# Between the two layers of a hybrid diffusion block: a new closing expert, gate rows in the routings, stores by SyncE, eight homes for the weight stream

## The reference, cut to what matters

```python
for l in range(DEPTH):
    ...
    h = modulate(rms_norm(x, g_pre_a), sh_a, sc_a)
    hc = modulate(rms_norm(xc, g_pre_a), csh_a, csc_a)
    mix, mix_c = token_mixers(h, hc, w_in[l], ...)
    x = x + gt_a * rms_norm(mix @ w_out[l], g_post_a)
    ...
    h = modulate(rms_norm(x, g_pre_f), sh_f, sc_f)
    x = x + gt_f * rms_norm(expert_choice_ffn(h, w_router[l], w_gate[l], w_up[l], w_down[l]), g_post_f)
    if update_ctx:
        ... the same for xc
```

## Time and profile before

| what | value |
|---|---|
| median of 3 runs (lowest, highest) | 2159.86 us (2159.2, 2161.35) |
| the profiled execution, its own time | 2164.66 us |
| its span, first to last instruction | 2162.9 us |
| PE busy / DVE busy / ACT busy / POOL busy | 89% / 25% / 22% / 8% |
| DMA over the span | 250 GB/s, 541.77 MB |
| mean granted TensorE clock | 0.952 of 2.4 GHz |

### The profile page before, as it was taken

The page is one execution under the profiler, slowest core; times in us unless marked ns, Lnnn a source line. Parts: engine busy times, 40 slices in busy tenths (PEclk is TensorE's granted clock), DMA queues, the critical chain, the costliest instruction groups (busy, mean ns, idle before and its releaser), DMA issues.

```text
span 2162.9 us, 25147 instructions
## 1 busy us (share of the span) xinstructions
PE 1916.5 (89%) x10460; PEld 892.7 (41%) x10460; DVE 545.7 (25%) x1168; ACT 473.5 (22%) x967; POOL 162.7 (8%) x230
## 2 busy tenths in 40 slices
PE   5998989999869999999997399879985989888885
PEld 2655545764423333333332255447632333332331
DVE  1021454761330000000000402456625011111113
ACT  4131113442311101111011513124421111111111
POOL 0000010100001011110101000011101000000000
PEclk9999989999979999999999699989997999999997
DMA  9221157002579999999999212110027999999994
GB/s 395 98 76 41 39 198 288 27 6 78 203 295 405 414 399 395 385 388 398 397 383 356 106 39 78 39 64 21 11 93 295 429 428 428 428 428 428 428 428 185
DMA packets 52750, 541.77 MB, mean 250 GB/s; under 512 B 6352, under 2 KB 8656, under 8 KB 23232
## 3 DMA queue, kind: packets, MB, share of 16 engines
q1 hardware_dynamic: 34400, 486.72, 54.9%
q0 software_dynamic: 18128, 53.95, 7.6%
q10 hardware_dynamic: 144, 0.01, 0.0%
HBM read 516.54 MB, written 24.12 MB: 250 GB/s over the span
## 4 chain that ended last, share of the span: by engine, by line
PE 72%; DMA 17%; DVE 6%; ACT 3%; issue 1%; POOL 0%; SPq 0%; DVEq 0%; POOLq 0%; ACTq 0%
DMA ring<-in_wstream 16%; PE ps L1694 15%; PE ps L1369 9%; PE ps L1757 7%; PE ps L1588 6%; PE ps L1702 5%; PE ps L1347 5%; PE ps L1536 3%; PE ps L1764 3%; PE ps L1474 2%; PE ps L1293 1%; PE ps L1339 1%; PE ps L1509 1%; PE ps L1502 1%; PE ps L1317 1%
## 5 line engine op out<-in xcount | busy, mean ns | idle before, releaser
L1694 PE MATMUL ps<-ring,work 128*64 128x512 f32 x2048 | 462.5, 604 | 38.4 <-DMA ring<-in_wstream 33.9
L1694 PEld LDWEIGHTS ps<-ring,work 128*64 128x64 f32 x2048 | 145.1, 139 | 349.9 <-issue 289.2
L1757 PE MATMUL ps<-big,work 128*64 128x512 f32 x1024 | 237.1, 605 | 3.1 <-ACT work L731 3.1
L1218 DVE TENSOR_TENSOR work<-glao,ps 128x512 f32<-128x512 f32 x32 | 22.0, 688 | 830.9 <-ACT glao L737 439.5
L1369 PE MATMUL ps<-hT,ring 128*128 128x512 f32 (+1 forms) x592 | 206.3, 507 | 1.9 <-DVE hT L880 1.4
L1369 PEld LDWEIGHTS ps<-hT,ring 128*128 128x128 f32 x592 | 112.0, 190 | 94.9 <-issue 86.4
L1588 PE MATMUL ps<-ring,hT 128*128 128x512 f32 x320 | 138.7, 592 | 0.0
L1757 PEld LDWEIGHTS ps<-big,work 128*64 128x64 f32 x1024 | 68.4, 138 | 140.2 <-issue 131.1
L1702 PE MATMUL ps<-ring,work 128*32 128x512 f32 x1024 | 119.8, 597 | 0.0
L1347 PE MATMUL ps<-ring,hT 128*128 128x384 f32 (+3 forms) x384 | 110.9, 450 | 0.0
L651 ACT ACTIVATE work<-ps,work 128x512 f32<-128x512 f32 (+2 forms) x120 | 82.0, 684 | 79.8 <-DVE work L1022 45.5
(11 more groups left out here) (256 smaller groups left out, 2020.4 us busy)
## 6 DMA issues: line engine op xcount, KB each, us to landing
ring<-in_wstream SPq DMA_DIRECT2D x166, 2048.0 KB, 12.7
big<-in_wstream SPq DMA_DIRECT2D x64, 2048.0 KB, 15.6
x_kept<-big POOLq DMA_DIRECT2D x14, 512.0 KB, 3.0
big<-x_kept POOLq DMA_DIRECT2D x14, 512.0 KB, 6.4
xn_lat<-big POOLq DMA_DIRECT2D x8, 512.0 KB, 10.8
big<-in_x_all SPq DMA_DIRECT2D x6, 512.0 KB, 6.4
work<-in_nat_bias POOLq DMA_DIRECT2D x16, 192.0 KB, 2.7
big<-in_x_all POOLq DMA_DIRECT2D x6, 512.0 KB, 6.9
```

The source lines that it names most:

```text
L1694: last = T.matmul(bank(m)[64 * h:64 * h + 64, :], XST[:, kc, e, 0:CAP_L], gate_up[j][:, kk, m * D + h * 512:m * D + (h + 1) * 512], start= ...
L1757: last = T.matmul(bank(3)[64 * g:64 * g + 64, :], HT[:, kc, 0:CAP_L], down[j][:, kc % 4, h * 512:(h + 1) * 512], start=kc == 0, stop=kc == ...
```

## The change

It has five parts.

1. **Gate rows of the expert stage** move into the routings: DVE builds the diagonals in layer 0 in `post_att`, in layer 1 at the end of `route`; PE multiplies and ACT copies them to `GROW_F` before the experts begin. PE waits for `grow_out` before its first gather transposes.
2. **Modulation units** are reordered: 12 under the attention, six (before: four) in layer 0's routing, of which the last two come after the indices are turned, none (before: two) between the layers.
3. **Layer 0's last expert** is written apart (`closing`): its context products come first, its context outputs are added on chip (`combine_ctx`), the context tiles are normed while PE computes the last latent down products; the latent outputs are added on chip too, together with the accumulators, by an identity product (`last_middle`). POOL scatters 15 experts, not 16, and reads the accumulators back before the last expert has ended. The next norm's scaling is folded into the transposing product (`turn_next`, with a scaled identity), two tiles at a time.
4. **Layer 1's experts** have eight homes for units (before six): the seventh in `big`, the eighth in two halves in `hT` and `work`. SP issues units 6 and 7 as soon as the first gathered rows are there. The programs of PE, ACT and SP for these experts are written out instead of looped. POOL reloads x for the closing norm when PE has used up unit 92 of 96 (before: all 96).
5. **Closing norm**: whole tiles of 1024 in one DVE addition, ACT's square-root table loaded beforehand, the result stored by SP.

```diff
-MOD_ROUTE = [[10, 11, 12, 13], [22, 23]]
-MOD_BOUND = [14, 15]
-MOD_ORDER = list(range(MOD_EARLY)) + MOD_ATT + MOD_ROUTE[0] + MOD_BOUND + MOD_ROUTE[1]
-MOD_GROUPS = [(0, 4), (4, 10), (16, 22), (10, 12), (12, 14), (14, 16), (22, 24)]
+MOD_ATT = list(range(4, 16))
+MOD_ROUTE = [list(range(16, 22)), [22, 23]]
...
+def laps(l, u):
+    if l < DEPTH - 1:
+        return u % SLOTS, u // SLOTS
+    return u % MORE, u // MORE + (NE if u % MORE < SLOTS else 0)
+def unit_used(l, n, j):
+    s, g = laps(l, SLOTS * n + j)
+    return ffn_used[s], g + 1
...
+for u in range(SLOTS, FFN_UNITS):
+    s, g = laps(l, u)
+    if g:
+        sp.wait_ge(ffn_used[s], g)
+    if s < MORE - 1:
+        sp.dma_start(ffn_slot(l, s), wstream[FFN_AT[l] + u, :, :]).then_inc(ffn_full[s], 16)
+    else:
+        for h in range(2):
+            sp.dma_start(home(l, s)[h], wstream[FFN_AT[l] + u, :, h * HALF:(h + 1) * HALF]).then_inc(ffn_full[s], 16)
...
+n = IN_AT[1] + i
+if i == 2:
+    for t in range(NLT):
...
             load(n)
+for t in range(NLT):
+    sp.wait_ge(sem("x_ready"), t + 1 + (DEPTH - 1) * NLT)
+    sp.dma_start(out[t * P:(t + 1) * P, :], X[:, t, :]).then_inc(sem("stored"), 16)
+sp.wait_ge(sem("stored"), 16 * NLT)
...
-for j in range(RING, SLOTS):
-    pool.wait_ge(ffn_used[j], (l + 1) * NE)
-for t in tiles(l):
+pool.wait_ge(*((ffn_used[4], NE) if ctx_too else unit_used(l, NE - 1, 2)))
...
+        scatter_add(2 * i + 1)
+for c in range(NCT):
+    pool.dma_start(X_CTX[:, c, :], xkeep[LAT + c * P:LAT + (c + 1) * P, :]).then_inc(sem(f"x_rows{NLT + c}"), 16)
+for c in range(NCT):
+    pool.wait_ge(sem(f"x_rows{NLT + c}"), 32)
+pool.wait_ge(sem("gather"), 3 * PAIRS)
+pool.wait_ge(sem("added"), ZERO_DMAS + 32 * (NE - 1))
 for t in tiles(l):
...
+        pool.dma_start(XN[:, t, :], src).then_inc(sem(f"x_rows{t}"), 16)
+    for t in range(NLT):
+        pool.wait_ge(sem(f"x_rows{t}"), ACC_READ)
+    x_again()
 else:
...
     modrow(n, SGL, bank(0))
+for j, n in enumerate(mods[4:]):
+    modrow(n, (SGL, SGC)[j], bank((0, 2)[j]))
+if not ctx_too:
+    act.wait_ge(sem("grow"), 1 + before("grow", l, "f"))
+    S.activation(GROW_F[0], ps[:, 2 * 512:4 * 512], ACT.Copy).then_inc(sem("grow_out"), 1)
 def picked(i, g):
     act.wait_ge(sem("gather"), i * (3 if ctx_too else 2) + (g + 1 + l * PER["gather"]))
...
+def closing(i, e):
+    act.wait_ge(sem("up_ctx"), 1)
+    S.activation(SGC[64:P, :], bank(2)[0:64, :], ACT.Silu).then_inc(sem("silu_ctx"), 1)
+    hidden_turned_ctx(i, e)
+    act.wait_ge(ffn_used[3], NE)
+    S.activation(SGL, bank(0), ACT.Silu).then_inc(sem("silu"), 1)
+    outputs_ctx(i, e).then_inc(sem("yev_ctx"), 1)
+    hidden_turned(i, e)
+    S.activation(AFM[:, 15:16], ones[:, 0:1], ACT.Sqrt)
+    output_square(l, NLT)
+    output_square(l, NLT + 1)
+    act.wait_ge(sem("cols"), 4 * (l + 1) + 2)
+    next_square(l, NLT)
+    outputs(i, e)
+    next_square(l, NLT + 1)
 def expert(i, e, last_pair):
...
+def post_middle(l):
+    output_square(l, 0)
+    output_square(l, 1)
+    act.wait_ge(sem("xT"), 1 + before("xT", l + 1, "a"))
+    h_next(range(KC // 2), 0)
+    next_square(l, 0)
+    h_next(range(KC // 2, KC), 0).then_inc(sem("h_ctx"), 1)
+    output_square(l, 2)
+    next_square(l, 1)
+    output_square(l, 3)
+    next_square(l, 2)
+    act.wait_ge(sem("xT"), 2 + before("xT", l + 1, "a"))
+    h_next(range(KC // 2, KC), 1).then_inc(sem("h_ctx"), 1)
+    next_square(l, 3)
+    act.wait_ge(sem("xT"), 4 + before("xT", l + 1, "a"))
+    h_next(range(KC // 2, KC), 2).then_inc(sem("h_ctx"), 1)
...
-    dve.wait_ge(sem("grow_out"), 1 + before("grow_out", l, half))
-    nxt = (l, "f") if half == "a" else (l + 1, "a")
-    if half == "f" and l == DEPTH - 1:
-        last_add(l, 0)
+def post_att(l):
...
+def new_x(i):
+    t = tiles(l)[i]
+    dve.wait_ge(sem("psq"), i + 1 + before("psq", l, "f"))
+    link(V.reciprocal(rs[:, t:t + 1], ss[:, t:t + 1]))
+    if t < NLT:
+        V.scalar_tensor_tensor(XN[:, t, :], ps[:, (t % 2) * D:(t % 2) * D + D], rs[:, t:t + 1], GROW_F[0], ALU.mult, ALU.mult)\
+            .then_inc(sem("y_used"), 1)
+        dve.wait_ge(sem("y_used"), t + 1 + before("y_used", l, "f"))
+        dve.wait_ge(sem(f"x_rows{t}"), X_AGAIN[l])
+        V.tensor_tensor(X[:, t, :], X[:, t, :], XN[:, t, :], ALU.add).then_inc(sem("x_ready"), 1)
     else:
-        dve.wait_ge(sem(f"x_rows{t}"), X_AGAIN[l])
-        done, n = ("x_ready", t + 1 + l * NLT) if t < NLT else ("xc_ready", t - NLT + 1)
-    V.tensor_tensor(X[:, t, :], X[:, t, :], GAIN_X, ALU.add).then_inc(sem(done), 1)
-    dve.wait_ge(sem(done), n)
-    if i and nxt[0] < DEPTH:
...
+new_x(0)
+new_x(1)
+normal(0)
+normal(1)
+for i in range(NCT, NT):
+    new_x(i)
+    if i > NCT:
+        normal(i - 1)
+dve.wait_ge(sem("xT"), 2 + before("xT", l + 1, "a"))
+h_next(range(KC // 2), 1)
+normal(NT - 1)
+dve.wait_ge(sem("xT"), 3 + before("xT", l + 1, "a"))
+h_next(range(KC // 2), 2)
...
+        mod_out(3, bank(1))
+    else:
+        dve.wait_ge(sem("mod_out"), 5)
+        gate_rows(l, "f")
 def ffn(l):
     ctx_too = l < DEPTH - 1
...
 last.then_inc(sem("logits"), 1)
 mods = MOD_ROUTE[l]
...
+for j, n in enumerate(mods[4:]):
+    mod_rows(n, bank((0, 2)[j]))
+for j, n in enumerate(mods[4:]):
+    mod_cols(n, (SGL, SGC)[j], bank(1))
+if l == DEPTH - 1:
+    gate_rows(l, "f")
...
-if ctx_too:
+    if ctx_too:
+        pe.wait_ge(ffn_full[j], i * 32 + 16 * (e + 1))
+    else:
+        s, g = laps(l, SLOTS * (2 * i + e) + j)
+        pe.wait_ge(ffn_full[s], (32 if s == MORE - 1 else 16) * (g + 1))
+if closing:
+    unit_in(0)
+    up_ctx(0)
+    up_lat(0).then_inc(ffn_used[0], 1)
+    unit_in(1)
+    up_lat(1)
+    up_ctx(1).then_inc(ffn_used[1], 1)
+    unit_in(2)
...
-        down_lat(1).then_inc(ffn_used[5], 1)
-pe.wait_ge(sem("mod_out"), (5, 7)[l])
+        down_lat(1).then_inc(used(5), 1)
+pe.wait_ge(sem("mod_out"), (4, 5)[l])
 pe.wait_ge(sem("xs_rows"), fetched(l, 1))
+pe.wait_ge(sem("grow_out"), 1 + before("grow_out", l, "f"))
 gather(0, 0)
 gather(0, 1)
...
+def last_middle(l):
+    def whole(t):
+        pe.wait_ge(sem(f"x_rows{t}"), ACC_READ)
+        if t == 0:
+            pe.wait_ge(sem("acc"), NCT)
+        elif t >= 2:
+            pe.wait_ge(sem("y_used"), t - 1 + before("y_used", l, "f"))
+        for h in range(2):
+            T.matmul(bank(2 * (t % 2) + h), ident, XN[:, t, h * 512:(h + 1) * 512], start=True, stop=False)
+        if t == 0:
+            pe.wait_ge(sem("yev"), NE)
+        for h in range(2):
+            r = slice(64 * h, 64 * h + 64)
+            last = T.matmul(bank(2 * (t % 2) + h), PT_L[0][r, t * P:(t + 1) * P], YL[1][r, :], start=False, stop=True)
+        last.then_inc(sem("comb"), 1)
+    def turn_next(i, b0):
+        t = tiles(l)[i]
+        pe.wait_ge(sem("xn"), i + 1 + before("xn", l + 1, "a"))
+        src = X[:, t, :] if t < NLT else X_CTX[:, t - NLT, :]
+        return [T.matmul(bank(b0, P, k * 2 * P + i % 2 * P), src[:, k * P:(k + 1) * P], NORM[t], start=True, stop=True) for k in range(KC)]
+    whole(0)
+    whole(1)
+    turn_next(0, 4)
+    turn_next(1, 4)[-1].then_inc(sem("xT"), 1)
+    whole(2)
+    whole(3)
+    pe.wait_ge(sem("h_ctx"), 1 + before("h_ctx", l + 1, "a"))
+    turn_next(2, 4)
+    turn_next(3, 4)[-1].then_inc(sem("xT"), 1)
+    pe.wait_ge(sem("y_used"), NLT + before("y_used", l, "f"))
+    turn_next(4, 0)
+    turned = turn_next(5, 0)
+    turned[KC // 2 - 1].then_inc(sem("xT"), 1)
+    turned[KC - 1].then_inc(sem("xT"), 1)
+    pe.wait_ge(sem("h_t"), 2 + before("h_t", l + 1, "a"))
+    pe.wait_ge(sem("h_ctx"), 3 + before("h_ctx", l + 1, "a"))
 pe.wait_ge(sem("silu_c"), 1)
 for n in range(MOD_EARLY + 1):
```

473 lines of the change are left out of this document (300 added, 173 removed).

## The result

The changed kernel takes 2124.91 us, median of 4 runs (2118.33 to 2127.46), against 2160.61 for the kernel before (2159.2 to 2163.09, 4 runs). The ratio is 0.9825, 95% interval 0.9806 to 0.9844. That is 35.7 us faster; 2124.5 had been predicted. The sum came out right with terms that did not: two are 1.4 and 2.5 us too good, one at the very end was put at 0.4 us and is worth 8, and part of what the stages gained is not in the medians.

What follows compares the result with a forecast made beforehand. PE bounds layer 0's experts, the weight stream layer 1's, a relay the passage between. Terms -27.4 + 3.5 - 9 + 0 - 2.5 = -35.4 us give 2129.3 profiled, 2124.5 median; 8 in 10: 2114 to 2141.

Steps and rivals of the forecast that it cites:

- Term 1: Passage between the layers: layer 1 starts sooner after layer 0's last expert, -27.4 us (-31 to -21).
- The walk: Forecast's step-by-step timing of engines through their written orders: passage's last modulation ends at 1201.1, tail takes 18.4 us.
- Rival A: Passage between the layers: context tiles come late because the accumulators' read-back waits longer, 7 to 18 us late; chance 0.15.
- Term 2: Layer 0's routing: added gate products and late modulation units delay the experts, +3.5 us (+1 to +7).
- Term 3: Layer 1's weight stream: units 6 and 7 go out when the gathered rows land, -9 us (-11 to -5).
- Term 4: Reload of x inside layer 1's weight stream: the last unit's delay is hidden, 0 us (0 to +2.5).
- slack 3.2 us. So nothing.: End of layer 1's stream: last unit in at about 2123.3, its down products at 2126.5, so a 1.6 us delay costs nothing.
- Term 5: Tail, the closing norm and stores: gate rows, copy and table load go away, -2.5 us (-4 to -1).
- SP issues in 0.33 what costs POOL 0.28 + 0.53: 0.4: Result stores at the end: issuing them from SP instead of POOL saves 0.4 us.
- B: Layer 1's stream: held by PE's releases or slow half units, the homes gain 0, total 2133.5; chance 0.12.
- D: Layer 0's routing costs nothing: late units' rows hide fully and the clock gives all back, 2119 to 2121; chance 0.08.
- C: Layer 1's experts: PE's written-out program must be fetched beside the full stream, +26 us, 2186; chance 0.03.

Runs made afterwards that it cites:

- The failed attempt to undo it: Changed kernel with layer 0's four routing gate products issued behind the affinities' transposes instead of ahead of them: median 2125.18 us, ratio 0.984.
- changed kernel again: The changed kernel run once more, unaltered, against the kernel before: median 2123.4 us, ratio 0.9829.

## Why the prediction was right

**Term 1, the passage: -27.4 forecast, -29.6 measured.** The mechanism was right; two sizes and one row were off. The walk had the accumulators' read at 1155.5 because it took the scatter as the only thing that the read waits for. Between them stand two reloads in POOL's own queue, behind the scatters and beside a full stream, which landed 7.2 us after the scatter; the walk gave them nothing, though the earlier trace rows warned of such prices. Rival A, which names this very cause, came true in part: the read was 7.6 us late, the last outputs left 3.5 us behind their products instead of 0.8, and 2.2 us of the stage hung on it. The turned tile, for which no row stood, cost 1.9 to 2.05 us, below the floor of 2.1: eight records of the row it was taken from, with two columns each, go slower than eight here. The modulations were priced from one that stood alone; four in a row take 1.93.

**Term 2, the routing: +3.5, measured +3.0.** Gate products 3.7 to 5.4 us (3.4 forecast; at half clock in part of it), transposes 5.3 to 7.0 us behind the logits (5.3 forecast), the gathered rows' turning 47.3 to 49.8 us behind the first turned tile where it was 43.7 and 45.1 (4.0 later in the mean, 6 forecast), and 1.3 us given back between there and the first product in eight of ten profiles, none in two (2.5 forecast). The first up products, which were to meet a warmer PE, took 6.0 to 6.6 us, as before (6.1 and 6.5). So both parts were smaller than forecast, and their difference fits. The failed attempt to undo it shows why the whole is less than its first part: the selection's delay runs alongside the modulation units, which PE must do there in any case.

**Term 3, the stream: -9, measured -7.6.** Right in place: the seventh unit goes out as the first gathered rows land. The first product is 2.2 us later (2.3 forecast). The size is off, and by more than the 1.4 us show. The last unit lands 461.7 us after the gather's issue (mean of the three kernels with x behind it), against 467.5 before: only 5.8 us of the 7.6 are the stream's. The seventh unit is asked for 10.8 us earlier, but the stream starts with 332 GB/s over its first 16 us, 3.6 us short of full, and 1.2 more are the second gather's bytes in it; 0.8 and 1.2 had been counted. That leaves 6.0. The other 1.8 us are luck as far as the forecast goes: before, the clock fell in the last down products (32 records in 8.8 us), and in these kernels it stays up (7.1).

**Term 4, the reload: 0, measured +2.5.** This step failed: "slack 3.2 us. So nothing." Two readings in it were off. The last unit of the kernel before does not land at 2123.3 but at 2124.4, 20.1 us after its issue at 2104.28. And its products began so late, at 2126.3, because PE was at half clock; kernel before, that unit's landing and PE's window:

```profile
DMA to landing us min/median/max: 20.1/20.1/20.1
```

```profile
2121.10:2126.30 5.20, 5.20 (x18) 1.62 (x20) 0.00 (x0) 0.00 (x0) 0.00 (x0) 0.67 0.27 113
```

So the slack was 1.9 us at that clock and, with 3.43 us instead of 5.2 for the products ahead, 0.1 at the full one. In a kernel whose PE stays warm there is none: without the reload the last unit lands at 2089.5 and PE takes it at 2089.6. So its whole delay shows: it lands 459.3 to 460.1 us after the first gathered rows with the reload inside the stream (five profiles), 457.0 to 457.8 without (three), 2.3 us. The Trainium skill, "DMA: Bandwidth & Descriptors", section "Queues, rings and completion order", has each DMA engine take the queues in turn, a packet at a time, from which the forecast worked out 4.9 us with equal packets; the rate of a gather beside the stream gave 1.6. Where both queues have work, the trace shows as many packets of one as of the other but not of one size (changed kernel again, 2084 to 2087: packets, MB):

```profile
q1 hardware_dynamic: 105, 0.79, 63.3%
q0 software_dynamic: 109, 0.44, 36.8%
```

That agrees with taking turns; the reload (q0) then gets 36% of the bytes, not half. The delay is smaller still than the 1.8 MB of the reload that move ahead of the last unit, 4.2 us at 428 GB/s, because the end of the stream leaves room: without the reload it carries 215 GB/s over its last 5 us.

**Term 5 and the end: -2.5, measured -2.4 and -8.0.** The walk of the tail was right to 0.1 us (18.4 forecast, 18.3); with it and the 0.4 the term would have been -2.7. "SP issues in 0.33 what costs POOL 0.28 + 0.53: 0.4" was the second step that failed. I compared issue costs and looked no further than the last row of the chain, at 2152.09; the span ended at 2162.9, and both numbers stood in front of me. Eleven microseconds behind a store that takes two to land were a question to ask.

**The sum.** The stages add up to -40.8 us (unrounded), 5.4 more than forecast: the end brought 8.0 where 0.4 was counted and terms 1 and 2 another 2.7, against 1.4 and 2.5 lost in terms 3 and 4 and 1.1 in layer 1's mixer and routing, whose cause stays open. The medians differ by only 35.7 and, in the second comparison, 37.7: 3 to 5 us of the stages' sum are not in them. So the mechanisms of terms 1 to 3 were right, but that the number came out within 0.4 us is luck: errors of 1 to 8 us cancelled. The profiled executions of the changed kernel are among its faster ones (2122.4 in 2118 to 2127, 2120.8 in 2121 to 2130) and that of the kernel before among its slower; with two profiles of before, whether its early stages lose something on average in the changed kernel stays open.

**The rivals.** B (the homes don't help) is refuted by the six-home kernel. D (the routing costs nothing) by 3.0 us in the mean; the shortest of ten profiles, 51.4, is above both of the kernel before. C (the written-out program must be fetched) did not come: 65 fetches instead of 55, one more than counted, and no stop of PE in layer 1's experts but for units and for the relay of hidden tiles.

```profile
q8 instruction: 65, 1.06, 0.2%
```

The Trainium skill, "Runtime: NRT & Kernel Launch", section "Instruction fetch mechanics", has straight-line code fetched ahead; the trace agrees, as far as ten fetches in 470 us can.

## What to carry to other kernels

Subtract the last row of the chain from the end of the span before forecasting anything about a program's end, look there for sequencer instructions, which busy times leave out, and let GpSimd finish early: give the last stores, and the wait for them, to another engine. A transfer that is off the path counts as soon as something on the path is queued behind it or shares the engines with the last needed load; ask of each "when does it have to be there", and issue it long before or right behind that load. Slack read from a trace may be half clock in disguise: recompute it at the clock that the changed kernel will have.

## What the runs showed of the hardware that was not expected

- GpSimd's program ends in a DRAIN of 7.0 to 7.9 us, and of 10.9 to 17.7 us where it follows four reloads still in flight, and the span ends after it (10.0 to 11.1 us from the last new tile when GpSimd waits for the stores, 8.4 when it only issues them, 3.0 when the DRAIN lies under the tail); worth 7.9 us of median in the kernel before, 6.5 in the changed one.
- A gather of 128 rows (0.5 MB) that takes 4.4 us to land with little else in flight takes 8.7 behind two units of 2 MB, and 11 in the full stream; two plain reloads of 0.5 MB each took 21 us, issued 1 us behind two scatters in the same queue, beside the stream.
- A plain reload and the stream, both with work, have as many packets in 3 us (109 and 105), of 4.0 and 7.5 KB.
- The first 570 us of programs that are alike up to there differ by up to 12 us between executions, with the granted clock of 300 to 400 us as the visible difference (0.81 and 0.91 against 0.92 and 1.00 in 50 us each, and with the kernel before's two profiles, in this order over thirteen of fourteen).
- Turning with a scaled identity on float32, eight products of 128 columns, takes 1.92 us a tile; the weight loads recorded with it take 3.65 of the 3.84 us of two.
